# Two mixture-of-experts stages of a trunk kernel: the down projection of a block issued one step after its gate and up

## The reference, cut to what matters

```python
    def run_block(args):
        idx, e = args
        xb = x_pad[idx]
        hid = jax.nn.silu(xb @ w_gate[e]) * (xb @ w_up[e])
        return hid @ w_down[e]
```

## Time and profile before

| what | us |
|---|---|
| median of 3 runs | 3452.34 (3441.14 to 3454.4) |
| span of the profiled execution, first to last instruction | 3440.8 |
| PE busy in the span | 2953.7 (86%) |
| expert stage of layer 0, first gate matmul to end of last down matmul | 1992.4 to 2494.5 |
| expert stage of layer 1, the same | 2773.0 to 3250.2 |

### The profile page before, as it was taken

The page is one execution under the profiler, slowest core; times in us unless marked ns, Lnnn a source line. Parts: engine busy times, 40 slices in busy tenths (PEclk is TensorE's granted clock), DMA queues, the critical chain, the costliest instruction groups (busy, mean ns, idle before and its releaser), DMA issues. The chain is left out here.

```text
span 3440.8 us, 53421 instructions
## 1 busy us (share of the span) xinstructions
PE 2953.7 (86%) x16322; PEld 2534.4 (74%) x16323; DVE 1949.2 (57%) x2787; ACT 1384.3 (40%) x2388; POOL 950.1 (28%) x894
## 2 busy tenths in 40 slices
PE   6999999999999999769999589999959589999700
PEld 5887788778877887658888489888849478889600
DVE  6548754876387638732211555576647777665433
ACT  5334333433343334321111145666624256666411
POOL 1013200320032003300000144465624256554332
PEclk8999999999999999979999689999979789999955
DMA  5323332323232323253222467798667569987555
GB/s 185 107 86 109 97 112 80 110 97 112 79 108 99 117 74 110 99 172 102 106 98 86 141 217 277 281 323 317 245 210 261 181 237 323 330 301 280 180 184 196
DMA packets 332189, 587.33 MB, mean 171 GB/s; under 512 B 23104, under 2 KB 206912, under 8 KB 332096
## 3 DMA queue, kind: packets, MB, share of 16 engines
q1 hardware_dynamic: 294944, 450.92, 38.3%
q0 software_dynamic: 37152, 135.28, 11.0%
HBM read 427.27 MB, written 158.86 MB: 170 GB/s over the span
## 5 line engine op out<-in xcount | busy, mean ns | idle before, releaser
L57 PE MATMUL ret_ps_p<-ret_w_hi,ret_x_hi 128*128 128x512 f32 x1536 | 606.7, 395 | 15.6 <-DVE ret_x_lo L1077 12.6
L59 PE MATMUL ret_ps_p<-ret_w_hi,ret_x_lo 128*128 128x512 f32 x1536 | 600.0, 391 | 0.0
L58 PE MATMUL ret_ps_p<-ret_w_lo,ret_x_hi 128*128 128x512 f32 x1536 | 599.2, 390 | 0.0
L1077 DVE TENSOR_TENSOR ret_x_lo<-hT,ret_x_hi 128x1024 fp32r<-128x1024 f32 x193 | 368.4, 1909 | 249.9 <-ACT ret_x_hi L1017 248.4
L57 PE MATMUL moe_ps_gu<-moe_gu_hi,moe_x_hi 128*128 128x256 f32 x1520 | 431.7, 284 | 3.5 <-DVE moe_x_lo L553 2.8
L58 PE MATMUL moe_ps_gu<-moe_gu_lo,moe_x_hi 128*128 128x256 f32 x1520 | 429.1, 282 | 0.0
L59 PE MATMUL moe_ps_gu<-moe_gu_hi,moe_x_lo 128*128 128x256 f32 x1520 | 429.1, 282 | 0.0
L985 POOL TENSOR_TENSOR ret_state_lo<-ret_state,ret_state_hi 128x1024 fp32r<-128x1024 f32 x68 | 176.6, 2597 | 838.2 <-ACT ret_state_hi L1007 838.2
L463 POOL TENSOR_TENSOR moe_dn_lo<-moe_raw_down,moe_dn_hi 128x1024 fp32r<-128x1024 f32 x128 | 366.5, 2881 | 17.7 <-ACT moe_dn_hi L498 16.9
L57 PEld LDWEIGHTS ret_ps_p<-ret_w_hi,ret_x_hi 128*128 128x128 f32 x1536 | 289.4, 188 | 77.2 <-DVE ret_x_lo L1077 14.4
L59 PEld LDWEIGHTS ret_ps_p<-ret_w_hi,ret_x_lo 128*128 128x128 f32 x1536 | 289.1, 188 | 61.7
(11 more groups left out here) (220 smaller groups left out, 5630.6 us busy)
## 6 DMA issues: line engine op xcount, KB each, us to landing
moe_raw_gate<-in_moe_w_gate SPq DMA_DIRECT2D x64, 1024.0 KB, 7.4
moe_raw_up<-in_moe_w_up SPq DMA_DIRECT2D x64, 1024.0 KB, 10.9
moe_raw_down<-in_moe_w_down SPq DMA_DIRECT2D x64, 1024.0 KB, 10.3
expert_rows<-moe_y POOLq DMA_DIRECT2D x95, 512.0 KB, 7.5
raw<-in_ret_w_in SPq DMA_DIRECT2D x20, 1024.0 KB, 9.0
qk_rows<-ret_qk_out SPq DMA_DIRECT2D x64, 256.0 KB, 2.1
ret_qk_out<-qk_rows SPq DMA_DIRECT2D x64, 256.0 KB, 3.0
gate_rows<-ret_gate SPq DMA_DIRECT2D x64, 256.0 KB, 2.0
```

The lines of the kernel that those rows point to most:

```text
L57: pe.matmul(out, x_hi, w_hi, start=first, stop=False)
L58: pe.matmul(out, x_hi, w_lo, start=False, stop=False)
L59: return pe.matmul(out, x_lo, w_hi, start=False, stop=last)
L1077: dve.tensor_tensor(x_lo[par][:, :, :], hT[:, :, ds(t * P, P)], x_hi[par][:, :, :].bitcast(F32), ALU.subtract).then_inc(x_split, 1)
```

## The change

- Gate and up of a block go into one PSUM bank: 24 matmuls of 512 columns. `ps_gu` is now one bank for all blocks, so the gate and up of block b wait until `hid` of block b-1 has been read out of it (`hid_ready`).
- The down projection of a block is issued one step later. PE's step b is: gate and up of b; both transposes of `hid` of b-1; the row transposes of b+1; down projection of b-1. After the loop a last transpose and down projection follow. The first two experts are taken out of the loop, since block 0 has no block before it.
- silu and `hid` are one instruction of 256 columns each instead of two of 128.
- ACT in step b: fills 0 to 3 (first block of an expert), `hT_hi` of b-1 twice, `x_hi` of b+1 twice, silu of b, left half of y of b-1, then a wait for the end of down b-1, and fills 4 and 5.
- DVE in step b: fills 0 to 3, `hT_lo` of b-1 twice, `x_lo` of b+1 twice, `hid` of b, right half of y of b-1.
- POOL in step b: gather of b+2, store of y of b-1, then fills 4 and 5.
- In the down projection the loop over column halves is now outside the loop over hidden halves. A one-element transfer at the head stands in for the store of step 0.

```diff
@@ POOL
+            def store(step):
+                pool.wait_ge(y_left, step + 1)
+                pool.wait_ge(y_right, step + 1)
+                pool.wait_ge(y_stored, 16 * step)
+                pool.sem_inc(y_free, 1)
+                b = step - 1
+                pool.dma_start(y_rows[ds(b * P, P), :], y[:, ds((step + 1) % 2, 1), :].rearrange("p a d -> p (a d)")
+                               ).then_inc(y_stored, 16)
...
-            def step(b, fill=lambda: None):
+            def step(b):
                 gather(b + 2)
-                fill()
-                pool.wait_ge(y_left, b + 1)
-                pool.wait_ge(y_right, b + 1)
...
+                if not is_first(b):
+                    store(b)
...
             def expert(e, par, more):
-                over_blocks(pool, e, lambda b: step(b, (lambda: split_down(e + 1, 1 - par)) if more else lambda: None), step)
+                def first(b):
+                    step(b)
+                    if more:
+                        for k in (4, 5):
+                            split_w(e + 1, 1 - par, k)
+                over_blocks(pool, e, first, step)
@@ ACT
             def block(b, fill):
...
+                if fill:
+                    for k in range(4):
+                        fill(k)
+                if not is_first(b):
+                    for j in range(FC):
+                        split_hT(b, j)
+                for j in range(2):
                     split_x(b + 1, j)
...
+                act.wait_ge(gu_ready, b + 1)
+                act.activation(silu[:, :], ps_gu[:, 0:FF], ACT.Silu).then_inc(silu_ready, 1)
+                if not is_first(b):
+                    leave(b)
+                if fill:
+                    if not is_first(b):
+                        act.wait_ge(y_summed, 2 * b + 2)
+                    for k in range(4, CHUNKS):
+                        fill(k)
@@ DVE
             def block(b, fill):
...
+                for k in range(4):
+                    fill(k)
+                if not is_first(b):
+                    for j in range(FC):
+                        split_hT(b, j)
+                for j in range(2):
                     split_x(b + 1, j)
...
+                dve.wait_ge(silu_ready, b + 1)
+                dve.tensor_tensor(hid[:, :, :].rearrange("p j n -> p (j n)"), silu[:, :], ps_gu[:, FF:2 * FF],
+                                  ALU.mult).then_inc(hid_ready, 1)
+                if not is_first(b):
+                    leave(b)
@@ PE
+            def gate_up(par, b):
                 pe.wait_ge(x_split, 2 * b + 2)
+                if not is_first(b):
+                    pe.wait_ge(hid_ready, b)
+                for c in range(DC):
+                    last = three_pass(pe, ps_gu[:, :], x_hi[:, c, :], x_lo[:, c, :],
+                                      gu_hi[par][:, c, :], gu_lo[par][:, c, :], c == 0, c == DC - 1)
+                last.then_inc(gu_ready, 1)
+
+            def transpose_hid(step):
...
+            def down(e, par, step):
                 pe.wait_ge(dn_split, 2 * (e + 1))
...
+            def block(par, b, before_e, before_par):
+                gate_up(par, b)
+                if not is_first(b):
+                    transpose_hid(b)
+                transpose_rows(b + 1)
+                if not is_first(b):
+                    down(before_e, before_par, b)
```

More of the change, by code:

```diff
@@ L337, in moe_phase @@
         x_lo = s.sb("x_lo", [P, DC, P], F32R)
[L338 removed]
+        silu = s.sb("silu", [P, FF])
         hid = s.sb("hid", [P, FC, P])
@@ L344, in moe_phase @@
         ps_x = s.ps("ps_x", [P, DC, P])
-        ps_gu = [s.ps(f"ps_gu{j}", [P, 4, P]) for j in range(FC)]
+        ps_gu = s.ps("ps_gu", [P, 2 * FF])
+        ps_rank = s.ps("ps_rank", [P, 2 * FF])
         ps_hT = [s.ps(f"ps_hT{j}", [P, 512]) for j in range(FC)]
@@ L406, in over_blocks @@
                 skip_runtime_bounds_check_because=in_bounds)
-            b0 = nc.s_assert_within(b0, 0, BLOCKS - 1, skip_runtime_bounds_check_because=in_bounds)
+            zero = isinstance(e, int) and e == 0
+            b0 = 0 if zero else nc.s_assert_within(b0, 1, BLOCKS - 1, skip_runtime_bounds_check_because=in_bounds)
             if ready:
@@ L415, in over_experts @@
         def over_experts(eng, body):
-            with eng.Fori(0, EXPERTS // 2 - 1) as i:
+            body(0, 0, True)
+            body(1, 1, True)
+            with eng.Fori(1, EXPERTS // 2 - 1) as i:
                 body(2 * i, 0, True)
@@ L503, in split_x, with split_hT, leave @@
                 act.activation(x_hi[:, c, :], ps_x[:, c, :], ACT.Copy).then_inc(x_hi_ready, 1)
-            def block(b, fill):
[L506 to L513, removed]
-                    split_x(b + 1, j)
[L515 to L520, removed]
+            def split_hT(step, j):
+                act.wait_ge(hT_ready, 2 * step + j + 1)
+                act.activation(hT_hi[:, j, :], ps_hT[j][:, 0:P], ACT.Copy).then_inc(hT_hi_ready, 1)
+            def leave(step):
+                act.wait_ge(y_summed, 2 * step + 1)
+                act.wait_ge(y_free, step)
+                s.passed(act)
+                act.activation(y[:, ds((step + 1) % 2, 1), 0:D // 2].rearrange("p a d -> p (a d)"), ps_y[:, 0:D // 2], ACT.Copy).then_inc(y_left, 1)
+            def block(b, fill):
+                if fill:
[5 more added lines that the diff above has]
+                for j in range(2):
+                    split_x(b + 1, j)
+                act.wait_ge(gu_ready, b + 1)
[7 more added lines that the diff above has]
+                        fill(k)
             def expert(e, par, more):
@@ L529, in first @@
                     else:
-                        block(b, lambda k: None)
-                over_blocks(act, e, first, lambda b: block(b, lambda k: None))
+                        block(b, None)
+                over_blocks(act, e, first, lambda b: block(b, None))
+            act.sem_inc(hT_hi_ready, FC)
+            act.sem_inc(y_left, 1)
             dispatch_scalar(act, lambda: [split_w(0, 0, 0, k) for k in range(CHUNKS)])
@@ L540, in _ @@
             over_experts(act, expert)
+            total = all_blocks(act)
+            for j in range(FC):
+                split_hT(total, j)
+            leave(total)
         @blk.vector
@@ L554, in split_x, with split_hT, leave @@
                                   ALU.subtract).then_inc(x_split, 1)
-            def block(b, fill):
[L557 to L565, removed]
-                    split_x(b + 1, j)
[L567 to L571, removed]
+            def split_hT(step, j):
+                dve.wait_ge(hT_hi_ready, 2 * step + j + 1)
+                dve.tensor_tensor(hT_lo[:, j, :], ps_hT[j][:, 0:P], hT_hi[:, j, :].bitcast(F32),
+                                  ALU.subtract).then_inc(hT_split, 1)
+            def leave(step):
+                dve.wait_ge(y_summed, 2 * step + 2)
+                dve.wait_ge(y_free, step)
+                s.passed(dve)
+                dve.tensor_copy(y[:, ds((step + 1) % 2, 1), D // 2:D].rearrange("p a d -> p (a d)"), ps_y[:, D // 2:D]).then_inc(y_right, 1)
+            def block(b, fill):
+                for k in range(4):
+                    fill(k)
+                if not is_first(b):
+                    for j in range(FC):
+                        split_hT(b, j)
+                for j in range(2):
+                    split_x(b + 1, j)
+                dve.wait_ge(silu_ready, b + 1)
[3 more added lines that the diff above has]
+                    leave(b)
             def expert(e, par, more):
@@ L585, in _ @@
             over_experts(dve, expert)
+            total = all_blocks(dve)
+            for j in range(FC):
+                split_hT(total, j)
+            leave(total)
         @blk.tensor
@@ L607, in block @@
+            def transpose_hid(step):
+                pe.wait_ge(hid_ready, step)
+                for j in range(FC):
                     pe.transpose(ps_hT[j][:, 0:P], hid[:, j, :], ident[:, :]).then_inc(hT_ready, 1)
-                    if j == 0:
-                        transpose_rows(b + 1)
+            def down(e, par, step):
                 pe.wait_ge(dn_split, 2 * (e + 1))
[L611 to L616, removed]
+                pe.wait_ge(y_left, step)
+                pe.wait_ge(y_right, step)
+                for n in range(2):
+                    cols = slice(n * D // 2, (n + 1) * D // 2)
+                    for c in range(FC):
+                        if n == 0:
+                            pe.wait_ge(hT_split, 2 * step + c + 1)
@@ L630, in _ @@
             over_experts(pe, expert)
+            total = all_blocks(pe)
+            transpose_hid(total)
+            down(EXPERTS - 1, 1, total)
 def norm_transpose_phase(nc, past, x, gain, hT, resident, raw, w_first):
```

42 lines of the change are left out of this document (18 added, 24 removed).

## The result

The changed kernel takes 3620.38 us (median of 4 runs, 3615.91 to 3621.51), the kernel before on the same chip 3446.74 (4 runs, 3440.54 to 3454.4): ratio 1.0498, interval 1.0469 to 1.0526. It is 5% slower. The direction and the engine that makes PE wait were as forecast; the wait and its price were longer, and the time lies 45 above the forecast and 10 above the range.

What follows compares the result with a forecast made beforehand. PE was taken to bound the expert stages, with 31 waits for `hid`. From 3452.3 us: one bank -6, stage ends +6, port +81, clock +43, sum +124, taken as 3575; range 3515 to 3610.

Steps and rivals of the forecast that it cites:

- The port exclusion: DVE and POOL weight subtractions exclude each other; pair steps take 13.8 instead of 11.2 us: 31 x 2.6 = +81.
- pair steps: Expert's first block right behind another first block, 31 of 95 blocks; forecast 13.8 us instead of 11.2.
- D: End of a down projection in a first block's step, followed by another first block; zero point of the forecast's chain.
- the clock: PE's clock halves after each pair step's pause: 1.4 us each, bounds 0 and 1.7, 31 x 1.4 = +43.
- the stages: The two expert stages were to grow from 502 and 477 us to about 560 and 545.
- Rival 1: Port exclusion as forecast, but the clock holds in pair steps: 3533 us, chance 0.23.
- Rivals 2 and 3: 2: DVE keeps the port through four fills, 3458, chance 0.08. 3: hid wait goes, nothing replaces it, 3406, 0.04.
- the pause: PE idle ahead of the down projection in each pair step, waiting on `hT_lo`: about 4 us, 31 times.
- when POOL is ready: Pair step: y copied until D+0.8, stored in 0.58, POOL ready at D+1.5; down projection starts at D+10.9.
- Other first blocks: First blocks outside pair steps: fills hidden; one-bank gate and up gains 0.1 us a block, -6 over 64 blocks.
- heads and tails: Ends of the two expert stages, with work exposed: about +3 us a stage, +6 in all, bounds 0 and +12.
- run of eight one-expert blocks: In layer 1, at 2785 to 2875 us: was to take over 110 us instead of 90.

Runs made afterwards that it cites:

- experiment 1: Changed kernel, but DVE also makes both down-weight low parts after its copy of y and POOL makes none: 3455.82 us, ratio to before 1.0023.
- experiments 5: Kernel of experiment 1, but ACT and DVE split the down pieces one expert later, behind the next expert's gates: 3400.81 us, ratio to before 0.9858.
- experiment 6: Kernel of experiments 5, but POOL makes the down weights' low parts, after its store of y: 3622.44 us, ratio to before 1.0503.
- experiment 3: Changed kernel plus 22 unread matmuls before the down projection in the first block of every expert but the first: 3715.18 us.
- experiment 2: Changed kernel, but POOL makes the down weights' low parts before it stores y, not after: 3570.31 us, ratio to before 1.036.

## Where the prediction was right, and which step failed

**Right: the place.** The port exclusion named from the earlier trace rows decided. It is shown from three sides: 5.50 beside POOL's pair in the changed kernel, 1.23 at most when POOL makes none (experiment 1), and 222 us between experiments 5 and 6. The Trainium skill's rule (SBUF — State Buffer, "Who interferes with whom"), that the later one blocks until the other's instruction has finished, agrees in the blocking. But the 5.50 against 1.21 holds two instructions of POOL, of which the second began 2.0 us after DVE had asked (2918.65; POOL's second at 2920.68); for that the measurement decides. The forecast, too, had one subtraction of DVE between POOL's two, and in the changed kernel there is none; either order costs the same sum. Of the 31 pair steps 30 start their down projection 12.3 to 12.5 after D (the other, at the head of layer 1, after 9.6); blocks outside them are at 9.54 and 9.65 where 9.6 was forecast.

**Right: the clock.** Its granted share in the stages is 0.91 and 0.90 (below 0.95 was forecast). Rival 1, that it holds, fell to the step's rest of 4.75 and to experiment 3. Rivals 2 and 3 fell to the pause of 5.5 and the subtraction of 5.50.

**The step that failed: when POOL is ready (42 of the 51 us missed).** The step "DVE copies half of y until D+0.8, POOL stores it (0.58) and is ready at D+1.5" gave a down start at D+10.9. Measured: the copy ends at D+1.2; between its end (2916.65) and the store's issue (2917.71) lie 1.06 us in which POOL's records show only semaphores and register work for the store's address, until 2917.14, and then nothing; then 0.58. POOL starts at D+2.84, the down projection at D+12.3. Its start moved by 3.96 against the kernel before, where the forecast had 2.6: 31 x 1.36 = +42. About 0.4 of this was a misreading: in the earlier trace rows the copy ends 1.2 after the start of gate and up (2842.77 against 2841.57), not 0.8. The rest is the way to the store. In the kernel before, the store's issue followed directly on a subtraction, and the same register work stands in POOL's records at 2843.4 to 2843.8, beside the subtractions ahead of it; the row's 0.58 was the engine's share alone. Experiment 2, in which nothing stands between ACT's pieces and POOL, measured 10.66. That the register work waits for y, and is not merely seen there, was not tried apart.

**Mis-sized: the clock's price (about +15).** "I take 1.4" out of bounds 0 to 1.7. Measured 1.88 by the step (2.87 to 4.75), 1.85 by experiment 3. The assumption behind 1.4 was one slow stretch of 3.4 us, part of it in the pause. Where one came, the price was close to that: in experiment 2, 17 pair steps with a stretch of 3.4 us have a rest of 4.35 (1.48 more than 2.87; one more, whose stretch runs on into the next step, has 4.02), and 12 with one of 6.8 us have 5.26 (2.39 more). In the changed kernel 28 of 30 have the stretch of 6.8, and a rest of 4.85 (1.98 more): the pause of 5.5 covers more of it than the one of 3.85 does. So the upper bound of 1.7, one whole stretch of the earlier trace rows, was too low, because the stretch can be twice as long.

**Mis-sized the other way (-6).** Other first blocks gained 0.37, not 0.1; part of it is waits that they had before (9.91 against 9.71 of the earlier trace rows). The heads and tails were forecast at +6 and measured +6.

So +124 became +175: +42 (POOL's start), +15 (clock), -6. The time lies only 45 above the forecast because the kernel before, with a fourth run, has its median at 3446.74, 5.6 below the 3452.34 that the forecast started from; that part is chance. The range failed because POOL's readiness, the start of a chain counted 31 times, stood in it as one value with no bound; the bounds went to the clock and the ends. With the 1.06 as an upper bound the range would have reached 3643. The bounds of port and clock were also added up wrong by a little: by their own terms they give 3558 to 3591, not 3560 to 3595.

**The forecast by its signs.** The stages were to be 560 and 545, and were 587 and 567. The run of eight one-expert blocks was to take over 110 us instead of 90; it takes 131 (2869.4 to 3000.5). The pause was to be about 4, and is 5.5.

## What to carry to other kernels

When work is moved behind a DMA issue or a wait, price the engine's way to it (registers, address, issue) as exposed time; a row in which that was hidden shows only the last part. A subtraction of two SBUF tiles on POOL costs DVE its whole length when DVE has one of the same kind to make: in a chain that both share, one engine making all of them (1.2 each) beats two in turn (2.4 for each of POOL's). And a pause on PE can bring the half clock into the work behind it: here 5.5 us idle cost 1.9 more.

## What the runs showed of the hardware that was not expected

Who goes next when both engines want the port is not settled by who asked first. In the changed kernel DVE asks for it 0.35 us after POOL's first subtraction begins, 2.1 before its end, and POOL's second still goes first: one DVE instruction of 5.50. In experiment 2 DVE asked 0.57 ahead of that end and went first (1.65), and so in experiment 6, where it had asked 2.4 ahead:

```profile
2951.75 5.74 POOL L480 TENSOR_TENSOR moe_dn_lo<-moe_raw_down,moe_dn_hi 128x1024 fp32r<-128x1024 f32 x2
2951.78 3.50 DVE L590 TENSOR_TENSOR moe_gu_lo<-moe_raw_up,moe_gu_hi 128x1024 fp32r<-128x1024 f32 x1
2955.20 3.37 DVE L590 TENSOR_TENSOR moe_gu_lo<-moe_raw_gate,moe_gu_hi 128x1024 fp32r<-128x1024 f32 x1
```

There the two take turns. POOL's place in its own queue does not decide it either: in both kernels its loop branch behind the two subtractions is on record before DVE asks (2917.9 before 2918.65; 2951.3 before 2951.78). What makes the difference stays open. It doesn't change the sum here: two of POOL's and four of DVE's must pass before `hT_lo` in either order.

The half clock's onset is not a matter of the pause alone. In experiment 1, six pair steps have a pause of 1.93 to 2.07 us ahead of the down projection; three of them got the half clock (rest of the step 4.0 to 4.5) and three did not, and none of those with 1.6 or less. The price of a pause of about 2 us is thus 0 or 1.1 to 1.6, and no run here tells which. Where it came in pair steps, it lasted 3.4 or 6.8 us.
